# Projecting all four tiles of the second gate inside the first attention instead of two ahead of the new keys

## The reference, cut to what matters

```python
z = h @ w_in
cq, ckv, kr, ga, qb, kb, vb, qi, ki, wi, gb, ma, mb = jnp.split(z, split_idx, axis=-1)
q  = rmsnorm(cq, g_qnorm) @ w_uq          # queries of the first attention
ckv = rmsnorm(ckv, g_kvnorm)              # latents: keys and values of the first attention
kn, va = mla_expand(ckv, w_ukv)
oa = mla_attend(...)                      # first attention ("mp", "ms" steps), gated by ga
ob = dsa_attend(...)                      # second attention over top-k keys ("dp", "ds"), gated by gb
ya = (oa * silu(ga)) @ w_oa
yb = (ob * silu(gb)) @ w_ob
m  = sigmoid(ma) * ya + sigmoid(mb) * yb
x  = x + gate * (m @ w_out)
```

## Time and profile before

| what | us |
|---|---|
| median of three runs | 1218.14 |
| profiled execution, its own time | 1217.27 |
| its span, first to last instruction | 1215.4 |
| TensorE busy in the span | 1143.7 |
| VectorE busy | 672.1 |
| ScalarE busy | 477.2 |
| GpSimd busy | 347.4 |

### The profile page before, as it was taken

How to read it: one execution, slowest core, us unless ns; L and a number is a source line. 1 busy time by engine, 2 the same in 40 slices (tenths; PEclk the granted TensorE clock), 3 DMA queues, 4 the chain that set the end, 5 groups by cost and what they waited for, 6 DMA issues and landing times.

```text
span 1215.4 us, 20113 instructions
## 1 busy us (share of the span) xinstructions
PE 1143.7 (94%) x7828; PEld 994.8 (82%) x7828; DVE 672.1 (55%) x1546; ACT 477.2 (39%) x1088; POOL 347.4 (29%) x213
## 2 busy tenths in 40 slices
PE   8999999999999999899979899999999999989995
PEld 5786995878888888699979499687888888878995
DVE  2828997742367764345363799954336622224535
ACT  3535345433433334323253634533244333333331
POOL 0430733121122222234343073403012321223431
PEclk9997999999999999999999799999999999998998
DMA  9442222111134333113444012221112411111342
GB/s 363 163 149 95 87 71 66 62 36 36 35 101 165 135 138 133 58 37 129 164 153 123 33 56 84 67 77 36 36 35 70 157 53 53 53 52 53 109 161 74
DMA packets 36670, 114.22 MB, mean 94 GB/s; under 512 B 5592, under 2 KB 8248, under 8 KB 35680
## 3 DMA queue, kind: packets, MB, share of 16 engines
q1 hardware_dynamic: 35264, 110.43, 27.5%
q10 hardware_dynamic: 1312, 2.51, 0.6%
HBM read 105.80 MB, written 7.12 MB: 93 GB/s over the span
## 4 chain that ended last, share of the span: by engine, by line
PE 81%; DVE 9%; ACT 5%; issue 2%; DMA 1%; POOL 1%; SPq 0%; POOLq 0%; DVEq 0%; ACTq 0%
PE pj L724 18%; PE pj L726 17%; PE pj L725 17%; PE po L1019 5%; PE ps L963 4%; PE turned L991 3%; PE ps L954 2%; PE pj L908 2%; DVE wide L1579 1%; ACT w_hi L1121 1%; POOL w_lo L1901 1%; PE ps L966 1%; PE pj L882 1%; DMA bias_p<-in_wts 1%; PE ps L836 1%
## 5 line engine op out<-in xcount | busy, mean ns | idle before, releaser
L724 PE MATMUL pj<-h_hi,w_hi 128*128 128x272 f32 x1704 | 506.4, 297 | 4.5 <-POOL w_lo L1901 3.6
L726 PE MATMUL pj<-h_lo,w_hi 128*128 128x272 f32 x1704 | 497.7, 292 | 0.0
L725 PE MATMUL pj<-h_hi,w_lo 128*128 128x272 f32 x1704 | 495.1, 291 | 0.0
L1901 POOL TENSOR_TENSOR w_lo<-ring,w_hi 128x1024 fp32r<-128x1024 f32 x107 | 260.2, 2432 | 580.4 <-ACT w_hi L1121 580.2
L724 PEld LDWEIGHTS pj<-h_hi,w_hi 128*128 128x128 f32 x1704 | 326.6, 192 | 8.0 <-POOL w_lo L1901 4.9
L725 PEld LDWEIGHTS pj<-h_hi,w_lo 128*128 128x128 f32 x1704 | 326.7, 192 | 0.2
L726 PEld LDWEIGHTS pj<-h_lo,w_hi 128*128 128x128 f32 x1704 | 325.5, 191 | 0.0
L1121 ACT ACTIVATE w_hi<-ring 128x1024 fp32r<-128x1024 f32 x107 | 113.7, 1062 | 112.7 <-PE pj L726 99.4
L1313 ACT ACTIVATE probs<-logit,negmax 128x128 f32<-128x128 f32 (+2 forms) x68 | 39.1, 575 | 210.4 <-DVE negmax L1650 196.7
L1650 DVE CUSTOM_DVE_ANT_0 logit<-ps,bias_p 128x128 f32<-128x128 f32 (+1 forms) x64 | 31.4, 491 | 148.8 <-PE ps L966 148.7
L1313 ACT ACTIVATE probs<-ps,negmax 128x128 f32<-128x128 f32 (+2 forms) x68 | 36.4, 536 | 142.7 <-DVE negmax L1641 125.6
(11 more groups left out here) (287 smaller groups left out, 1555.5 us busy)
## 6 DMA issues: line engine op xcount, KB each, us to landing
ring<-in_wts SPq DMA_DIRECT2D x150, 512.0 KB, 3.6
wide<-in_xT SPq DMA_DIRECT2D x4, 1088.0 KB, 7.2
wide<-in_wts SPq DMA_DIRECT2D x6, 512.0 KB, 15.7
ring<-in_wts SPq DMA_DIRECT2D x6, 384.0 KB, 2.9
x_between<-wide ACTq DMA_DIRECT2D x8, 272.0 KB, 3.4
wide<-x_between SPq DMA_DIRECT2D x2, 1088.0 KB, 5.7
bias_p<-in_wts SPq DMA_DIRECT2D x4, 512.0 KB, 14.7
bias_p<-bias_rows SPq DMA_DIRECT2D x1, 2048.0 KB, 7.8
```

The source lines that it names most:

```text
L724: pe.matmul(out, hi, h_hi[:, k, half(b)], start=(k == first), stop=False)
L725: pe.matmul(out, lo, h_hi[:, k, half(b)], start=False, stop=False)
L726: return pe.matmul(out, hi, h_lo[:, k, half(b)], start=False, stop=(k == stop))
L1901: pool.tensor_tensor(lo, w(splits[n]), hi.bitcast(F32), ALU.subtract).then_inc(s_wlo, 1)
```

## The change

`EARLY_GB` goes from 2 to 0. No `gb` tile is projected between the latents' squares and the new keys, and `fillers` begins with all eight `gb` jobs. `fill_places` then spreads 18 jobs over the first attention: `gb` in steps 0, 1, 3, 5, 7, 9, 11, 13, `qb` in 15, 16, 18, 20, 22, 24, 26, 28, `kb` in 30 and 32. Steps 34 and later keep theirs. In the order of loads, tiles 2 and 3 of `gb` move from ahead of `uk` to behind `ukt`; tiles 0 and 1 stay ahead of `uk`, because `prepare` splits them before the latents' norm. The loops over `range(EARLY_GB)` on TensorE, ScalarE and GpSimd become empty.

```diff
-EARLY_GB = 2
+EARLY_GB = 0
...
-    t += [("cq", n, P, 1024) for n in range(3)] + [("gb", n, P, 1024) for n in range(4)]
+    t += [("cq", n, P, 1024) for n in range(3)] + [("gb", n, P, 1024) for n in range(EARLY_GB + 2)]
     t += [("uk", 0, P, 1024), ("uv", 0, P, 1024)] + [("uq", n, P, 768) for n in range(3)]
     t += [("ukt", n, 64, 1024) for n in range(2)]
```

## The result

The changed kernel takes 1234.28 us (median of 5 runs, 1225.02 to 1237.2) beside 1218.1 us of the kernel before (5 runs, 1214.22 to 1225.27): ratio 1.0135, 95% interval 1.0099 to 1.0171. Run again beside the experiments, it took 1235.31 against 1216.79 us, ratio 1.0131 (1.0096 to 1.0166). The forecast was 1228.5 us in a range of 1221 to 1235, slower by 0.85%; the direction and most of the mechanism held, the size was 10.4 us where 16.2 and 18.5 were measured. The first median lies 0.7 us inside the upper bound of the range and the second 0.3 us beyond it, so that it fell inside was in part luck.

The account below looks back on a forecast made before the run. TensorE, 81% of the chain, was taken to bound the kernel. Per layer 12.44 for moved jobs, -0.3 of waits, -6.97 for an earlier start gave +5.2, twice +10.4: median 1228.5 us, range 1221 to 1235.

Parts of the forecast that it names:

- The old place covers a wait: Ahead of the keys: the early jobs cover a 7.7 us wait for the normed latents and overshoot it by 4.6.
- The bank wait of 2.40 goes, and the table load is hidden: At the fourth key job TensorE's 2.40 us wait goes; ScalarE's 1.28 us table load moves to idle time before the first exponential.
- One low stretch over the keys, worth 1.81: After 7.7 us of idling, one stretch at half clock over the keys, costing 1.81 us a layer.
- bound of 3.6: Over the keys: the slow end of the clock's price, a low stretch twice as long, 1.8 us more than counted.
- The attention hides nothing: four jobs at 3.11 us: In the first attention, each moved job adds 3.11 us, four 12.44 us a layer.
- the rival that read room off the weight loads' busy share: Attention has 23.3 us a layer free, so the moved jobs vanish there: 1204.2 us; chance 0.03.
- Waits in the attention, net -0.3: First attention: waits of 1.6 us go at early steps, 1.3 come behind steps 17 and 29, 0.3 less a layer.
- The clock in the attention unchanged: At step 0 and behind the expansion, low clock stays 3.4 us each, adding nothing to the sum.
- every span from step 34 on unchanged: Behind the first attention, from step 34 on, every span was to last as long as before.
- The clock stays low: Rival: behind the wait ahead of the keys 12.2 us run at half rate, +4.3 a layer, 1237.0 us; chance 0.14.
- the clock's middle value between two ends: Over the keys: one low stretch, between none (1.8 us less) and twice as long (1.8 more) a layer.

Follow-up runs that it names:

- e1: Against the kernel before: one early `gb` tile instead of two, three moved into the first attention; 1213.36 us beside 1215.81, ratio 0.9986.
- e5: Kernel before with the four early `gb` jobs cut from 24 matmuls to 3 at the old place; 1205.52 us beside 1217.92, ratio 0.9905.
- e3: Changed kernel plus 15 unread matmuls in TensorE's wait ahead of the keys; 1227.59 us beside 1215.81 for the kernel before, ratio 1.0098.
- e11: Kernel before, two tiles early, with the first attention's 14 jobs placed anew; 1216.08 us beside 1216.24, ratio 0.9995.
- e6: Changed kernel with the four moved jobs cut from 24 matmuls to 3; 1219.05 us beside 1217.92 for the kernel before, ratio 1.0011.
- e9: Changed kernel with jobs in steps 16, 20, 24, 28 moved to 17, 21, 25, 29; 1223.35 us beside 1216.79 for the kernel before.
- e8: Changed kernel with one job a layer moved from step 11 to 12, behind the expansion; 1228.49 us beside 1216.79 for the kernel before.
- e2: Kernel before with ScalarE's eight rotary-key copies put ahead of the early tiles' gates; 1215.59 us beside 1215.81, ratio 0.998.

## Why the prediction was right in direction and short in size

- *The old place covers a wait.* Right. The wait is 7.37 us idle by the trace, 7.7 from the last squares; e1 and e5 show that work there is free up to the normed latents and not behind them.
- *The bank wait of 2.40 goes, and the table load is hidden.* Right: keys in one piece, copies done 1.5 us before they start, the load ahead of the exponential.
- *One low stretch over the keys, worth 1.81.* Mis-sized. The keys took 9.72 us, and 9.97 and 9.30 us in the two layers of the other profile; at full clock they take 6.97 (e3). So 2.3 to 3.0, inside the bound of 3.6 that I had set but above the value taken. The low stretch was 10.2 us long and began in the idling:

```profile
171.10:181.30 10.20, 6.03 (x7) 0.50 0.00 1
```

  The line is of the profile of 1225.02 us, whose keys start at 175.27. The row nearest to the wait was not a good price for it: a longer idling brought a longer stretch. Nor does the bank wait of 2.40 always bring the low clock that the earlier trace rows has behind it. In layer 1 of e11 it is there, and the fourth key job takes 1.98 us instead of 3.58:

```profile
778.07 1.98 PE L875 MATMUL pj<-ckv,ring 128*128 128x512 f32 x4 [2.40 <-ACTq L1270]
```

- *The attention hides nothing: four jobs at 3.11 us.* Right in kind (e6), and the rival that read room off the weight loads' busy share is refuted: the matmuls' waits were nearly all the room. The Trainium skill (Trainium Kernel Development and Optimization, Performance Expectations) calls weight-load busy time a good measure of how close a kernel is to its limit, and matmul busy time a bad one. Read as room for more work, that did not hold in this stretch: loads were 80% busy, and 12.4 us of added jobs lengthened it by 11.8 us at equal clock (125.4 against 113.6, which are 131.5 and 117.0 less half of the time in which TensorE was busy at low clock, 12.2 and 6.8 us).
- *Waits in the attention, net -0.3.* The places were right, all of them: steps 17, 21, 25 and 29 wait, 1, 3 and 5 do not. The price was not: by e9 a listed 0.65 is 1.1. Five waits of this kind were listed before and four after, so with 1.1 for each the attention would have grown by some 11.3 us, by the forecast 12.15; it was 11.8 at equal clock. The error in the price moved the sum by less than 1 us a layer.
- *The clock in the attention unchanged.* This is the step that failed. I priced the low stretches at step 0 and behind the expansion as staying 3.4 us each; they were 3.4 and 10.2 in both layers. Of the 10.2 us TensorE was busy for 8.73, so the longer stretch costs (8.73 - 3.4) / 2 = 2.7 us a layer, 5.4 in all. With `gb` out of step 12, the expansion's 32 small matmuls, a score, a transpose and a wait of 1.5 us stand in a row with no projection between. By the table under e8 that makes up one half of the 6.8 us of added low clock. The other half is the moment: in the kernel before the clock fell 3.3 us after the expansion's first matmul, in this profile 2.1 after it. The first half goes with the change in all traces; no run shows whether the second does. Both low stretches of 3.4 us in the profile of the kernel before were the shortest that this place shows.
- The sum corrected: at equal clock +11.8 - 4.5 - 2.5 = +4.8 us a layer, 9.6 for two (10.4 forecast, in which the clock cost the same as before); +2.2 from the keys' clock, +5.4 from the attention's. That makes 17.2, the sum of the stages above. The forecast also had every span from step 34 on unchanged; +3.3 us of low clock stood there in this profile and only part of it in the other.
- Of the rivals, none happened. "The clock stays low" came nearest: low for 10.2 us, but over 4.2 to 4.9 us of idling too, where it costs nothing. The chances had the outcome, slower by over 1%, at 0.28. I had put the clock's middle value between two ends as if both were alike; but the change makes two of TensorE's light stretches longer, so the slow end was the likelier.

What stays open: what decides the moment at which the clock falls. One kernel with one order has it differently in its two layers (in e2, 3.0 us after the expansion's first matmul in layer 0 and 0.4 in layer 1), and so layers and runs differ by 3 to 7 us of low clock at one place. No run set that moment at will.

## What to carry to other kernels

Work parked ahead of a wait is free up to the moment at which the wait would end, and costs in full wherever else the engine is bound; so move only what stands behind that moment, and look at what the parked work delays on the engines that finish it (here eight copies behind the gates of two tiles). Spread filler work by where its cover is short, not evenly: after long reductions with short work beside them (e9) and right behind runs of small matmuls, where a job shortened the low clock by 3.4 us (the table under e8). And when an edit wins a few microseconds by the trace and nothing by the clock on the wall, multiply each run's span by its mean TensorE clock before judging it. Add back half of the time that TensorE idled at low clock: here the product alone puts the changed kernel 2.9 us above the kernel before, and the idling hides some 6 more.

## What the runs showed of the hardware that was not expected

- TensorE's clock fell behind stretches in which the profile calls it fully busy: the 32 matmuls of 32 columns of the expansion (L1028) have 1.00 of the clock ahead of them and 0.50 during or right behind them in both layers of all fourteen traces. How long the low stretch was, 3.4 to 10.2 us, went with the moment of the fall and with what followed (the table under e8).
- Runs of one kernel differ in low-clock time by 30 us and more (e2: 72 to 105 us; the changed kernel: 101 to 131), which alone moves the time by 1%.
- An idle time listed at 0.65 us cost 1.1 us (e9).
- The clock can stay low while TensorE has no idle time at all: 10.2 us at 0.50, busy for 10.20, in layer 1 of e2.
